# Second pair of layers: eight attention units scored and paired between the value projection's products

## The chip, the cores and the metric

The kernel runs on one core of a Trainium2 chip. The metric is the device time of one execution in microseconds (us); of several runs the median is taken. TensorE (PE) multiplies, VectorE (DVE) and ScalarE (ACT) read its sums from PSUM, GpSimd (POOL) works from SBUF alone, SyncE (SP) starts most transfers.

## The reference, cut to what matters

The program runs two blocks of two layers each. The change touches only the second block, `hybrid_layer`, on 512 positions of 1024 features. Its attention has three kinds of heads: six of kind a (three dilated windows with a bias), four of kind b (the difference of two softmaxes, with a bias), six of kind c (latent queries and keys, with rope).

```
def probs(q, k):                     # kind b
    s = jnp.einsum('bqhd,bkhd->bhqk', sl(q), k) * scale + bias
    return jax.nn.softmax(jnp.where(causal, s, -jnp.inf), axis=-1)
a = probs(q1, k1) - lam * probs(q2, k2)
lam = exp(sum(lf[0] * lf[1])) - exp(sum(lf[2] * lf[3])) + lam_init
out = jnp.einsum('bhqk,bkhd->bqhd', a, v)
```

After attention come the output projection with a layer norm, and a gated feed-forward with a second one. All is in float32.

## The kernel before

Every weight tile is split into a high part (`w_hi`, by ACT, line 759) and a low part (`w_lo`, by POOL, line 705), and each product of a projection is three matmuls (lines 1255 to 1257). SP loads the raw tiles into three slots; a slot is free once its low part is made. There are two slots for split tiles; `split_next()` in ACT's program splits the next tile of a fixed list.

Each engine runs its own program in order and waits on semaphores. A layer of the second block runs so on PE: the projections c, bq, bk and bv; three tiles of a's queries and keys (`("a", j)`), with the transposes of the latent rows among them; a's value projection `("av", kh)`, two halves of four row blocks with 12 matmuls of 384 columns each; the tile `up` (rope queries, c's keys `kn`, the rotation at line 1792, c's queries `qn`, c's values `vc`); the attention loop; the output projection.

The attention loop has 80 units, listed by `units2()`. A unit is one head and one block of 128 queries against n = 128, 256, 384 or 512 keys. Kind b takes two units each, 16 pairs in all. The order is two pairs, then the other 14 pairs spread among 34 units of kinds c and a, then 14 more of a. Of a unit the engines do, each one step or more behind the last:

- PE scores it into one of three PSUM banks, 0, 4 and 6 (line 1838; one matmul for kind b, two for c and a);
- DVE adds the mask or bias strip, writes the buffer `sc2`, and finds the least value (line 2455);
- ACT takes the exponential and its sum (line 1176);
- for the second unit of a pair, DVE scales it and adds the first to it (lines 2465 to 2467);
- four steps after its score PE transposes it (line 1849), ACT copies that to `pt2` (line 1170), and two ranks later PE multiplies it with the values (line 1823); DVE scales the result into `ao` (line 2438).

Banks for the transposes are 2, 1, 3, 5 and 7 in turn. Four of the five `sc2` buffers lie in the high part of the split slot that tile `up` uses, and the fifth in its low part, so the loop cannot write them before `up`'s products are done. Kind c's scores wait for the rope (`s_roped`, DVE line 2407), for the rope keys copied to all heads (`s_kr_all`, POOL lines 733 and 736) and for ACT's copies of `qn` (line 1157).

ACT, before the loop, copies what PE projects: `va` (line 1145), the rope rows (lines 1146 and 1150), then issues six strip loads from its own queue (line 1120), copies `kn` and `qn` (line 1157) and `vc` (line 1160), and takes the exponential for lambda (line 1162). At loop steps 8 and 10 it splits the two halves of the first tile of the output projection. The bias strips of kind b lie in slots 0 to 3 of `strips`, those of kind a in slots 4 to 8, and one in `strips_g`.

Of the kernel before, what the change touches and what calls it, by code (L numbers as in the profile page):

```python
# [16 lines left out]
ALU = mybir.AluOpType  # L17
# [114 lines left out]
def _program(nc, I, out, seen):  # L132
    ctx = ExitStack()
    with ctx:
# [421 lines left out]
        SLOT_ORDER = (3, 0, 2, 1)  # L556

        def units2():
# [40 lines left out]
        STEPS = len(UNITS) + N_B - 1  # L599
        LAST = len(RANKS) - 1  # L600
# [142 lines left out]
        def _(act):  # L743
# [336 lines left out]
            for l in range(DEPTH):  # L1080
# [53 lines left out]
                for j in range(3):  # L1134
                    if j == 2:
                        for i in range(3):
                            act.wait_ge(s_lat.sem, s_lat.at((y, i)))
                            act.activation(cq_hi[:, i, :] if i < 2 else ckv_hi[:], tmp_c[:, i % 2, :], ACT.Copy).then_inc(s_hi.sem, s_hi.nth((y, "c", i)))
                    a_out(2 * j)
                    a_out(2 * j + 1)  # L1140
                    split_next()
                split_next()
# [8 lines left out]
                for h in range(A_HEADS):  # L1151
                    load_strip(h, s_strips)
# [8 lines left out]
                act.wait_ge(s_lam_sums.sem, s_lam_sums.at(y))  # L1161
                act.activation(lam[:, 2:4], lam[:, 0:2], ACT.Exp).then_inc(s_lam_exp.sem, s_lam_exp.nth(y))
                for step in range(STEPS):
# [7 lines left out]
                    if step < len(UNITS):  # L1171
                        u = UNITS[step]
                        n, p_ = u["n"], sc2[step % N_B]
                        total = small[:, 1, step % 8:step % 8 + 1] if u["second"] else sums[:, u["sum"]:u["sum"] + 1]
                        act.wait_ge(s_scored.sem, s_scored.at((y, step)))
                        act.activation(p_[:, 0:n], p_[:, 0:n], ACT.Exp, bias=small[:, 0, step % 8:step % 8 + 1], scale=-1.0,
                                       accum_out=total).then_inc(s_probs.sem, s_probs.nth((y, step)))
# [53 lines left out]
        def _(pe):  # L1231
# [451 lines left out]
            for l in range(DEPTH):  # L1683
# [49 lines left out]
                for j in range(3):  # L1733
# [5 lines left out]
                    if j == 1:  # L1739
                        for i, b in enumerate((5, 7, 0, 2)):  # L1740
# [9 lines left out]
                            m.then_inc(s_lat_t.sem, s_lat_t.nth((y, i)))  # L1750
                for kh in range(2):
# [74 lines left out]
                pe.wait_ge(s_b_lo.sem, s_b_lo.at((y, "bk", 1)))  # L1826
                for step in range(STEPS):
                    if step < len(UNITS):
                        u, b = UNITS[step], S_BANKS[step % N_S]
                        pe.wait_ge(*emptied[b])  # L1830
                        emptied[b] = s_scored.after((y, step))
                        if u["kind"] == "c":
                            pe.wait_ge(s_roped.sem, s_roped.at((y, 1)))
                            pe.wait_ge(s_kr_all.sem, s_kr_all.at((y, u["head"])))
                            pe.wait_ge(s_proj.sem, s_proj.at((y, "qn", 2, 1)))
                        if u["kind"] == "a":
                            pe.wait_ge(s_padded.sem, s_padded.at(y))
                        pe.matmul(ps[:, b, 0:u["n"]], u["q"], u["k"], start=True, stop=True).then_inc(s_scores.sem, s_scores.nth((y, step)))  # L1838
                    r = turns(step)
                    if r is not None:  # L1840
# [7 lines left out]
                        for j in range(len(UNITS[i]["vs"])):  # L1848
                            m = pe.transpose(ps[:, b, P * j:P * j + P], sc2[i % N_B][:, P * j:P * j + P], ident[:])  # L1849
# [107 lines left out]
        def _(dve):  # L1957
# [404 lines left out]
            for l in range(DEPTH):  # L2362
# [35 lines left out]
                m.then_inc(s_lam_sums.sem, s_lam_sums.nth(y))  # L2398
                R = slice(HD, QC)
# [41 lines left out]
                dve.wait_ge(s_strips_b.sem, s_strips_b.at(y))  # L2441
                for st in range(STEPS):
                    if st < len(UNITS):
                        u = UNITS[st]
                        n = u["n"]
                        if st >= N_B and UNITS[st - N_B]["first"]:
                            dve.wait_ge(s_paired.sem, s_paired.at((y, st - N_B + 1)))
                        elif st >= N_B:
# [3 lines left out]
                        if u["kind"] == "a":  # L2452
                            dve.wait_ge(s_strips.sem, s_strips.at(y))
                        dve.wait_ge(s_scores.sem, s_scores.at((y, st)))
                        V.tensor_tensor_reduce(sc2[st % N_B][:, 0:n], ps[:, S_BANKS[st % N_S], 0:n], u["mask"], 1.0, 3.0e38, ALU.add, ALU.min,  # L2455
                                               small[:, 0, st % 8:st % 8 + 1]).then_inc(s_scored.sem, s_scored.nth((y, st)))
                    i = st - 2
                    if st == 2:
                        dve.wait_ge(s_lam_exp.sem, s_lam_exp.at(y))
                        step(V.scalar_tensor_tensor(lam[:, 4:5], lam[:, 3:4], lam[:, 2:3], lam_c[:, 0:1], ALU.subtract, ALU.add))  # L2460
                    if 0 <= i < len(UNITS) and UNITS[i]["second"]:
                        u = UNITS[i]
                        n, ratio = u["n"], small[:, 2, i % 8:i % 8 + 1]
                        dve.wait_ge(s_probs.sem, s_probs.at((y, i)))
                        step(V.reciprocal(ratio, small[:, 1, i % 8:i % 8 + 1]))
                        step(V.tensor_scalar(ratio, ratio, sums[:, u["sum"]:u["sum"] + 1], lam[:, 4:5], ALU.mult, ALU.mult))
                        V.scalar_tensor_tensor(sc2[i % N_B][:, 0:n], sc2[i % N_B][:, 0:n], ratio, sc2[(i - 1) % N_B][:, 0:n],
                                               ALU.mult, ALU.add).then_inc(s_paired.sem, s_paired.nth((y, i)))
# [82 lines left out]
```

## Time and profile before

| | us |
|---|---|
| median of 3 runs | 2019.71 (2019.66 to 2033.64) |
| the profiled execution | 2029.09 |
| its span | 2027.3 |

The profile covers one execution. Times in it run from the start of the span. A row of busy time names an engine and the share of a stretch; PEclk is the clock granted to PE as a share of 2.4 GHz, so 0.50 is 1.2 GHz. A row of the timeline gives the start, the duration, the engine, the line, what is written and read, and in square brackets how long the engine had been idle before and whose work released it. Matmuls overlap at their ends. The attention of the two layers lies at about 849 to 960 us and 1494 to 1605 us.

### The profile page before, as it was taken

The numbers are of one execution on the slowest core, as the hardware profiler recorded it, in microseconds if no ns is written. First come the engines' busy times: TensorE is split into PE (matmuls) and PEld (weight loads), VectorE is DVE, ScalarE is ACT, GpSimd is POOL, SyncE is SP. The second block draws the span as 40 slices with busy tenths as digits, with TensorE's granted clock in tenths as the row PEclk, the third lists the DMA queues.
The fourth block names the chain that finished last, engine by engine and source line by source line (L and its number), as shares of the span: only waits on it lengthen the run. The fifth ranks groups of instructions, "written<-read, shape, count | busy, mean of one in ns | idle before, by whom it ended". The sixth has DMA issues, their size and how long they took to land.

```text
span 2027.3 us, 26898 instructions
## 1 busy us (share of the span) xinstructions
PE 1957.9 (97%) x10454; PEld 1654.0 (82%) x10454; DVE 794.4 (39%) x1830; ACT 827.2 (41%) x1571; POOL 701.1 (35%) x552
## 2 busy tenths in 40 slices
PE   8999999989999999999999999999998999999997
PEld 4898879878779888777888888888877788888886
DVE  3656546452637344367511111027247551111004
ACT  3221268364248456567233222125467523232211
POOL 1523330125450244300544444444420135444441
PEclk9999989999999999999999999999979999999999
DMA  9554320112340024200333333323320133333321
GB/s 275 174 163 149 117 84 2 32 42 83 104 151 33 18 83 126 99 22 16 90 95 92 104 95 114 104 76 104 105 99 1 43 84 104 90 97 104 120 88 42
DMA packets 198117, 183.72 MB, mean 91 GB/s; under 512 B 31686, under 2 KB 166204, under 8 KB 197992
## 3 DMA queue, kind: packets, MB, share of 16 engines
q1 hardware_dynamic: 191960, 170.67, 27.6%
q10 hardware_dynamic: 6032, 11.33, 1.7%
q8 instruction: 85, 1.39, 0.3%
q14 instruction: 40, 0.33, 0.1%
HBM read 179.86 MB, written 5.40 MB: 91 GB/s over the span
## 4 chain that ended last, share of the span: by engine, by line
PE 85%; DVE 6%; ACT 4%; POOL 2%; issue 2%; DMA 1%; ACTq 0%; SPq 0%; DVEq 0%
PE ps L1255 22%; PE ps L1257 22%; PE ps L1256 22%; PE ps L1341 3%; PE ps L1823 3%; PE ps L1838 3%; POOL w_lo L705 2%; PE ps L1849 2%; PE ps L1327 2%; PE ps L1315 2%; PE ps L1372 1%; PE ps L1289 1%; DVE sc L2455 1%; ACT w_hi L759 1%; PE ps L1276 1%
## 5 line engine op out<-in xcount | busy, mean ns | idle before, releaser
L705 POOL TENSOR_TENSOR w_lo<-raw,w_hi 128x512 fp32r<-128x512 f32 (+1 forms) x518 | 679.3, 1343 | 1222.1 <-ACT w_hi L759 1222.0
L759 ACT ACTIVATE w_hi<-raw 128x1024 fp32r<-128x1024 f32 (+2 forms) x261 | 258.2, 1037 | 279.2 <-PE ps L1257 212.7
L1255 PE MATMUL ps<-g_hi,w_lo 128*128 128x512 f32 (+1 forms) x928 | 348.6, 376 | 1.5 <-POOL w_lo L705 1.5
L1256 PE MATMUL ps<-g_lo,w_hi 128*128 128x512 f32 (+1 forms) x928 | 347.7, 375 | 0.0
L1257 PE MATMUL ps<-g_hi,w_hi 128*128 128x512 f32 (+1 forms) x928 | 347.7, 375 | 0.0
L1255 PEld LDWEIGHTS ps<-g_hi,w_lo 128*128 128x128 f32 x928 | 174.7, 188 | 33.7 <-issue 1.7
L1257 PEld LDWEIGHTS ps<-g_hi,w_hi 128*128 128x128 f32 x928 | 174.7, 188 | 31.1
L1256 PEld LDWEIGHTS ps<-g_lo,w_hi 128*128 128x128 f32 x928 | 174.8, 188 | 31.1
L1255 PE MATMUL ps<-h_hi,w_lo 128*128 128x512 f32 (+1 forms) x496 | 180.3, 363 | 4.0 <-DVE h_lo L1972 2.3
L2516 DVE TENSOR_TENSOR tmp_f<-ps,tmp_f 128x512 f32<-128x512 f32 x44 | 30.4, 691 | 370.8 <-PE ps L1257 370.8
L1256 PE MATMUL ps<-h_lo,w_hi 128*128 128x512 f32 (+1 forms) x496 | 174.8, 352 | 0.0
L1257 PE MATMUL ps<-h_hi,w_hi 128*128 128x512 f32 (+1 forms) x496 | 174.7, 352 | 0.0
L1255 PE MATMUL ps<-w_hi,hid_lo 128*128 128x512 f32 x352 | 137.2, 390 | 0.0
L1256 PE MATMUL ps<-w_lo,hid_hi 128*128 128x512 f32 x352 | 137.0, 389 | 0.0
L1257 PE MATMUL ps<-w_hi,hid_hi 128*128 128x512 f32 x352 | 137.0, 389 | 0.0
L1212 ACT ACTIVATE hid_hi<-tmp_f 128x512 fp32r<-128x512 f32 x44 | 27.8, 632 | 237.1 <-DVE tmp_f L2516 237.1
L1255 PE MATMUL ps<-w_hi,g_lo 128*128 128x512 f32 (+3 forms) x320 | 114.3, 357 | 5.3 <-POOL w_lo L705 4.1
L2486 DVE SCALAR_TENSOR_TENSOR res<-res,ps 128x512 f32<-128x512 f32 x32 | 21.9, 684 | 244.9 <-PE ps L1257 244.7
L1257 PE MATMUL ps<-w_hi,g_hi 128*128 128x512 f32 (+3 forms) x320 | 112.9, 353 | 0.0
L1256 PE MATMUL ps<-w_lo,g_hi 128*128 128x512 f32 (+3 forms) x320 | 112.5, 352 | 0.0
L1255 PEld LDWEIGHTS ps<-h_hi,w_lo 128*128 128x128 f32 x496 | 93.9, 189 | 20.8 <-issue 7.3
L1256 PEld LDWEIGHTS ps<-h_lo,w_hi 128*128 128x128 f32 x496 | 94.0, 189 | 14.1 <-issue 2.2
(277 smaller groups left out, 3494.9 us busy)
## 6 DMA issues: line engine op xcount, KB each, us to landing
raw<-in_w_in SPq DMA_DIRECT2D x30, 1024.0 KB, 5.4
raw<-in_w_mod SPq DMA_DIRECT2D x24, 1024.0 KB, 6.4
raw<-in_w_gate SPq DMA_DIRECT2D x44, 512.0 KB, 4.0
raw<-in_w_up SPq DMA_DIRECT2D x44, 512.0 KB, 5.2
raw<-in_w_down SPq DMA_DIRECT2D x22, 1024.0 KB, 4.8
raw<-in_w_out SPq DMA_DIRECT2D x8, 1024.0 KB, 5.0
strips<-bias_rows ACTq DMA_DIRECT2D x18, 256.0 KB, 3.9
raw<-in_w_in SPq DMA_DIRECT2D x16, 256.0 KB, 4.5
```

The costliest lines, as they stand in the source:

```text
L705: pool.tensor_tensor(w_lo[:, i % SPLIT, a:e], raw_of(what)[:, a:e], w_hi[:, i % SPLIT, a:e].bitcast(F32), ALU.subtract).then_inc(s_tile_lo ...
L759: act.activation(w_hi[:, i % SPLIT, a:b], raw_of(what)[:, a:b], ACT.Copy).then_inc(s_tile_hi.sem, s_tile_hi.nth((what, n)))
L1255: pe.matmul(o, lhs[1], rhs[0], start=first, stop=False)
L1256: pe.matmul(o, lhs[0], rhs[1], start=False, stop=False)
L1257: return pe.matmul(o, lhs[0], rhs[0], start=False, stop=last)
L1315: m = pe.matmul(ps_flat[:, o0 + CTX + col:o0 + CTX + col + k.shape[1]], q, k, start=j == 0, stop=j == len(products) - 1)
L1327: m = pe.transpose(ps_flat[:, o0 + P * j:o0 + P * j + P], s_[:, i % n_b, P * j:P * j + P], ident[:])
L1341: m = pe.matmul(ps_flat[:, o0:o0 + HD], turned, v, start=j == 0, stop=j == n - 1)
L1823: m = pe.matmul(ps[:, b, 0:HD], pt2[r % N_P][:, P * j:P * j + P], v, start=j == 0, stop=j == len(u["vs"]) - 1)
L1838: pe.matmul(ps[:, b, 0:u["n"]], u["q"], u["k"], start=True, stop=True).then_inc(s_scores.sem, s_scores.nth((y, step)))
L1849: m = pe.transpose(ps[:, b, P * j:P * j + P], sc2[i % N_B][:, P * j:P * j + P], ident[:])
L2516: V.tensor_tensor(tmp_f[:, 2 + j % 2, :], ps[:, 2 * ((j + 2) % 4) + 1, :], tmp_f[:, j % 2, :], ALU.mult).then_inc(s_glu.sem, s_glu.nth((y, ...
```

## The change

The first four pairs (units 0 to 7, head 0 of kind b) leave the loop. PE scores them behind the row blocks of the value projection, DVE and ACT make and pair their probabilities meanwhile, and these lie in the five strip slots of kind a instead of `sc2`. The exponential for lambda moves ahead of them. The loads of a's strips move from ahead of ACT's `kn` copies into loop steps 14 to 19, one a step, and the split of the output projection's first tile from steps 8 and 10 to 24 and 26. The loop starts at step 5, with units 8, 9 and 10 scored ahead of it; the remaining 12 pairs are spread over the same 34 other units.

```diff
         SLOT_ORDER = (3, 0, 2, 1)
+        EARLY = 8
+        EARLY_AT = (0, 1, 2, 3, 4, 0, 2, 4)
+        EARLY_AMONG = ((0, 1), (2,), (3,), (4,), (5,), (6,), (7,), ())
...
-            u = pairs[0] + pairs[1]
+            u = [x for two in pairs[:EARLY // 2] for x in two]
...
-            for n, two in enumerate(pairs[2:]):
-                upto = (n + 1) * 34 // len(pairs[2:])
+            for n, two in enumerate(pairs[EARLY // 2:]):
+                upto = (n + 1) * 34 // len(pairs[EARLY // 2:])
...
+        FROM = N_B
+        LOADS_FROM = EARLY + N_B + 1
+        def probs_of(i):
+            return strips[:, B_HEADS + EARLY_AT[i], :] if i < EARLY else sc2[i % N_B]
```

ACT (`exp2` is the body of the old loop's exponential, over `probs_of`):

```diff
+                act.wait_ge(s_lam_sums.sem, s_lam_sums.at(y))
+                act.activation(lam[:, 2:4], lam[:, 0:2], ACT.Exp).then_inc(s_lam_exp.sem, s_lam_exp.nth(y))
+                for i in range(EARLY - 4):
+                    exp2(i)
                 split_next()
                 for t in range(XT):
+                    exp2(EARLY - 4 + t)
                     act.wait_ge(s_mm.sem, s_mm.at((y, "av", 1, t)))
...
-                for h in range(A_HEADS):
-                    load_strip(h, s_strips)
...
-                act.wait_ge(s_lam_sums.sem, s_lam_sums.at(y))
-                act.activation(lam[:, 2:4], lam[:, 0:2], ACT.Exp).then_inc(s_lam_exp.sem, s_lam_exp.nth(y))
-                for step in range(STEPS):
+                for step in range(FROM, STEPS):
...
+                    if EARLY <= step < len(UNITS):
+                        exp2(step)
+                    if LOADS_FROM <= step < LOADS_FROM + A_HEADS:
+                        load_strip(step - LOADS_FROM, s_strips)
-                    if step == 8:
+                    if step == 24:
                         split_next((0,))
-                    if step == 10:
+                    if step == 26:
                         split_next((1,))
```

PE (`score(i)` is the body of the old loop's score, with its waits):

```diff
+                pe.wait_ge(s_b_lo.sem, s_b_lo.at((y, "bk", 1)))
                 for kh in range(2):
...
                         m.then_inc(s_mm.sem, s_mm.nth((y, "av", kh, t)))
+                        for i in EARLY_AMONG[XT * kh + t]:
+                            score(i)
...
-                for step in range(STEPS):
-                    if step < len(UNITS):
...
+                for i in range(EARLY, EARLY + N_S):
+                    score(i)
+                for step in range(FROM, STEPS):
+                    if EARLY + N_S <= step < len(UNITS):
+                        score(step)
...
-                            m = pe.transpose(ps[:, b, P * j:P * j + P], sc2[i % N_B][:, P * j:P * j + P], ident[:])
+                            m = pe.transpose(ps[:, b, P * j:P * j + P], probs_of(i)[:, P * j:P * j + P], ident[:])
```

DVE (`scored(i)` and `pair(i)` are the bodies of lines 2455 and 2465 to 2467; this stands ahead of the rope):

```diff
+                dve.wait_ge(s_strips_b.sem, s_strips_b.at(y))
+                for i in range(4):
+                    scored(i)
+                dve.wait_ge(s_lam_exp.sem, s_lam_exp.at(y))
+                step(V.scalar_tensor_tensor(lam[:, 4:5], lam[:, 3:4], lam[:, 2:3], lam_c[:, 0:1], ALU.subtract, ALU.add))
+                for i in range(4, EARLY):
+                    if i > 4:
+                        dve.wait_ge(s_paired.sem, s_paired.at((y, (1, 3, 5)[i - 5])))
+                    scored(i)
+                    pair(2 * (i - 4) + 1)
                 R = slice(HD, QC)
...
-                for st in range(STEPS):
+                for st in range(EARLY, STEPS):
```

## Rows read from the trace of the kernel before

**Rows 1.** The page: span, busy shares, granted clock in 40 slices.

```profile
span 2027.3 us, 26898 instructions
PE 1957.9 (97%) x10454; PEld 1654.0 (82%) x10454; DVE 794.4 (39%) x1830; ACT 827.2 (41%) x1571; POOL 701.1 (35%) x552
PEclk9999989999999999999999999999979999999999
```

**Rows 2.** Busy by stretch: length, PE, PEld, DVE, ACT, POOL; PEclk, DMA, GB/s.

```profile
848.75:854.56 5.81, 2.42 (x8) 1.05 (x7) 4.17 (x13) 5.72 (x15) 3.92 (x6) 1.00 0.00 0
854.56:871.64 17.08, 16.54 (x62) 13.81 (x63) 10.09 (x41) 10.52 (x30) 5.00 (x4) 0.50 0.18 62
871.64:960.35 88.71, 80.50 (x570) 66.67 (x570) 64.44 (x262) 64.17 (x197) 0.00 (x0) 1.00 0.01 1
1493.56:1496.24 2.68, 1.13 (x6) 0.57 (x5) 2.65 (x6) 2.64 (x6) 2.62 (x4) 1.00 0.01 3
1496.24:1516.70 20.46, 19.17 (x66) 14.88 (x67) 11.84 (x50) 13.85 (x40) 6.28 (x7) 0.50 0.14 52
```

**Rows 3.** Timeline of PE where the first attention starts.

```profile
848.75 0.80 PE L1838 MATMUL ps<-bk,bq 128*128 128x512 f32 x3
850.83 0.33 PE L1838 MATMUL ps<-bk,bq 128*128 128x128 f32 x1 [1.28 <-DVE small L2455]
...
855.10 1.12 PE L1849 MATMUL ps<-ident,sc 128*128 128x128 f32 x4 [2.37 <-DVE sc L2467]
```

**Rows 4.** Timeline of DVE: the rope and the first pair.

```profile
841.90 0.69 DVE L2402 TENSOR_TENSOR tmp_c<-ps,sin 128x512 f32<-128x512 f32 x1 [25.98 <-PE ps L1792]
...
847.66 2.38 DVE L2407 TENSOR_TENSOR qc<-qr,tmp_c 32x512 f32<-32x512 f32 x2
...
854.30 0.75 DVE L2467 SCALAR_TENSOR_TENSOR sc<-sc,small,sc 128x512 f32<-128x512 f32 x1
```

**Rows 5.** Timeline of ACT from the last split ahead of the loop.

```profile
827.90 1.90 ACT L759 ACTIVATE w_hi<-raw 128x1024 fp32r<-128x1024 f32 x2 [6.28 <-PE ps L1257]
...
839.00 2.26 ACTq L1120 DMA_DIRECT2D strips<-bias_rows  x5
...
841.78 3.68 ACT L1157 ACTIVATE kc<-ps 64x512 f32<-64x512 f32 x6 [2.20 <-PE ps L1257]
...
849.19 1.64 ACT L1160 ACTIVATE vc<-ps 128x384 f32<-128x384 f32 x4
850.85 1.28 ACT L1162 ACT_TABLE_LOAD   x1
```

**Rows 6.** Busy by stretch, as rows 2: the value projection.

```profile
820.00:836.00 16.00, 16.00 (x94) 16.00 (x93) 0.00 (x0) 5.00 (x8) 8.54 (x7) 1.00 0.25 78
```

**Rows 7.** Lines of DVE: count, ns least/median/most, first and last start, forms.

```profile
L2455 DVE CUSTOM_DVE_ANT_0 sc<-ps,strips x104: 280/486/692, 850.1 to 1593.4; 128x512 f32<-128x512 f32 x26, 128x128 f32<-128x128 f32 x26, 128x384 f32<-128x384 f32 x26, 128x256 f32<-128x256 f32 x26
L2467 DVE SCALAR_TENSOR_TENSOR sc<-sc,small,sc x32: 351/552/752, 854.3 to 1579.5; 128x512 f32<-128x512 f32 x8, 128x128 f32<-128x128 f32 x8, 128x384 f32<-128x384 f32 x8, 128x256 f32<-128x256 f32 x8
```

**Rows 8.** Transfers of b's strips, issued from 787.7: KB each, median us to landing.

```profile
strips<-bias_rows ACTq DMA_DIRECT2D x4, 256.0 KB, 5.3
```

**Rows 9.** Timeline of POOL: low parts of `up`, rope keys.

```profile
829.04 4.75 POOL L705 TENSOR_TENSOR w_lo<-raw,w_hi 128x512 fp32r<-128x512 f32 x4 [4.06 <-ACT w_hi L759]
...
847.71 1.79 POOL L733 TENSOR_TENSOR kc<-qr,tmp_c 32x512 f32<-32x512 f32 x1 [13.92 <-DVE qr L2403]
```

**Rows 10.** Chain that ended last: a c score at full clock.

```profile
877.20 0.91 PE ps L1838 x2
```

**Rows 11.** Busy by stretch, as rows 2, where PE paused elsewhere.

```profile
278.00:282.00 4.00, 0.74 (x5) 0.46 (x4) 4.00 (x11) 3.44 (x8) 1.82 (x1) 0.89 0.37 111
438.00:440.00 2.00, 0.03 (x1) 0.04 (x1) 1.07 (x3) 1.78 (x5) 0.05 (x1) 1.00 0.00 0
610.00:614.00 4.00, 1.79 (x14) 1.38 (x13) 4.00 (x13) 3.64 (x10) 1.55 (x1) 1.00 0.31 66
```

**Rows 12.** Timeline of PE behind the pause at 437 us.

```profile
439.97 1.64 PE L1391 MATMUL ps<-ident,xn 128*128 128x128 f32 x13 [2.84 <-DVE xn L2070]
```

More of the change, by code:

```diff
@@ L1141, in _, with exp2 @@
                     split_next()
+                def exp2(i):
+                    u = UNITS[i]
+                    p_ = probs_of(i)[:, 0:u["n"]]
+                    total = small[:, 1, i % 8:i % 8 + 1] if u["second"] else sums[:, u["sum"]:u["sum"] + 1]
+                    act.wait_ge(s_scored.sem, s_scored.at((y, i)))
+                    act.activation(p_, p_, ACT.Exp, bias=small[:, 0, i % 8:i % 8 + 1], scale=-1.0,
+                                   accum_out=total).then_inc(s_probs.sem, s_probs.nth((y, i)))
+                act.wait_ge(s_lam_sums.sem, s_lam_sums.at(y))
+                act.activation(lam[:, 2:4], lam[:, 0:2], ACT.Exp).then_inc(s_lam_exp.sem, s_lam_exp.nth(y))
+                for i in range(EARLY - 4):
+                    exp2(i)
                 split_next()
                 for t in range(XT):
+                    exp2(EARLY - 4 + t)
                     act.wait_ge(s_mm.sem, s_mm.at((y, "av", 1, t)))
@@ L1750, in _, with score @@
                             m.then_inc(s_lat_t.sem, s_lat_t.nth((y, i)))
+                def score(i):
+                    u, b = UNITS[i], S_BANKS[i % N_S]
+                    pe.wait_ge(*emptied[b])
+                    emptied[b] = s_scored.after((y, i))
+                    if u["kind"] == "c":
+                        pe.wait_ge(s_roped.sem, s_roped.at((y, 1)))
+                        pe.wait_ge(s_kr_all.sem, s_kr_all.at((y, u["head"])))
+                        pe.wait_ge(s_proj.sem, s_proj.at((y, "qn", 2, 1)))
+                    if u["kind"] == "a":
+                        pe.wait_ge(s_padded.sem, s_padded.at(y))
+                    pe.matmul(ps[:, b, 0:u["n"]], u["q"], u["k"], start=True, stop=True).then_inc(s_scores.sem, s_scores.nth((y, i)))
+                pe.wait_ge(s_b_lo.sem, s_b_lo.at((y, "bk", 1)))
                 for kh in range(2):
@@ L2398, in _, with scored, pair @@
                 m.then_inc(s_lam_sums.sem, s_lam_sums.nth(y))
+                def scored(i):
+                    u = UNITS[i]
+                    n = u["n"]
+                    dve.wait_ge(s_scores.sem, s_scores.at((y, i)))
+                    V.tensor_tensor_reduce(probs_of(i)[:, 0:n], ps[:, S_BANKS[i % N_S], 0:n], u["mask"], 1.0, 3.0e38, ALU.add, ALU.min,
+                                           small[:, 0, i % 8:i % 8 + 1]).then_inc(s_scored.sem, s_scored.nth((y, i)))
+                def pair(i):
+                    u = UNITS[i]
+                    n, ratio = u["n"], small[:, 2, i % 8:i % 8 + 1]
+                    dve.wait_ge(s_probs.sem, s_probs.at((y, i)))
+                    step(V.reciprocal(ratio, small[:, 1, i % 8:i % 8 + 1]))
+                    step(V.tensor_scalar(ratio, ratio, sums[:, u["sum"]:u["sum"] + 1], lam[:, 4:5], ALU.mult, ALU.mult))
+                    V.scalar_tensor_tensor(probs_of(i)[:, 0:n], probs_of(i)[:, 0:n], ratio, probs_of(i - 1)[:, 0:n],
+                                           ALU.mult, ALU.add).then_inc(s_paired.sem, s_paired.nth((y, i)))
+                dve.wait_ge(s_strips_b.sem, s_strips_b.at(y))
[8 more added lines that the diff above has]
+                    pair(2 * (i - 4) + 1)
                 R = slice(HD, QC)
@@ L2439, in rows_out2 @@
                                     ALU.mult).then_inc(s_o_out.sem, s_o_out.nth((y, r)))
-                dve.wait_ge(s_strips_b.sem, s_strips_b.at(y))
-                for st in range(STEPS):
+                for st in range(EARLY, STEPS):
                     if st < len(UNITS):
                         u = UNITS[st]
-                        n = u["n"]
-                        if st >= N_B and UNITS[st - N_B]["first"]:
+                        if st >= EARLY + N_B and UNITS[st - N_B]["first"]:
                             dve.wait_ge(s_paired.sem, s_paired.at((y, st - N_B + 1)))
-                        elif st >= N_B:
+                        elif st >= EARLY + N_B:
                             dve.wait_ge(s_turned.sem, s_turned.at((y, UNITS[st - N_B]["rank"])))
@@ L2453, in _ @@
                             dve.wait_ge(s_strips.sem, s_strips.at(y))
[L2454 to L2468, printed above, removed]
+                        scored(st)
+                    if EARLY <= st - 2 < len(UNITS) and UNITS[st - 2]["second"]:
+                        pair(st - 2)
                     if turns(st) is not None and turns(st) >= 3:
```

19 lines of the change are left out of this document (1 added, 18 removed).

## The prediction

> **What bounds the kernel now.** I read the page first: PE is busy for 97% of the span, and its clock is granted in full but for a few slices [rows 1]. So a gain must take idle time or half-clock time from PE, or PE's work itself. The change removes no product, so only the first two are open. The lowest slice, a 7, is the thirtieth (1470 to 1520 us). The busy times by stretch show that it holds the head of layer two's attention, and that layer one's head, which a slice at 9 hides, is the same [rows 2]. Layer one: from 848.75 us PE is busy for 2.42 of 5.81 us; at 854.56 the clock falls to half and stays there for 17.08 us, while PE is busy for 16.54 of them; from 871.64 to 960.35 it is at full clock and busy for 80.50 of 88.71. Layer two has the same order, with 20.46 us at half clock.
>
> The timelines say why. PE ends the last `vc` product and issues three scores; then it idles 1.28 us for the first bank and 2.37 us for the first paired probabilities [rows 3]. DVE cannot take the first score sooner, since it is in the rope until 850.04 (847.66 + 2.38) [rows 4]. ACT is late as well: its `vc` copies end at 850.83, and 1.28 us of table load come before the first exponential [rows 5]. Meanwhile DVE had been idle for 25.98 us before the rope [rows 4]: that is the place into which the change moves work.
>
> **What the head costs in layer one.** From 848.75 to 871.64 are 22.89 us. PE's work in them, in time at full clock, is 2.42 + 16.54/2 = 10.69. Half clock costs 8.27, idle time 3.39 + 0.54 = 3.93. Layer two: 2.68 + 20.46 = 23.14 us, with 1.13 + 19.17/2 = 10.72 of work [rows 2].
>
> **The eight early scores.** They have 2 × (512 + 128 + 384 + 256) = 2560 columns, one matmul each. 94 products of 384 columns fill 16.00 us, 0.17 each [rows 6]; at 320 columns a score that gives 8 × 0.17 × 320/384 = 1.13. Three of them (512, 512, 128) took 0.80 [rows 3], and the other five, none above 384 columns, at most 0.17 each, so no more than 1.65. I take 1.2. They leave the head and lengthen the value projection by the same, so everything behind it starts 1.2 later.
>
> **What hides their other parts.** DVE needs 8 × 0.49 + 4 × 0.55 = 6.1 us by the medians [rows 7], with the small steps behind each some 9 by my estimate, inside its 25.98 idle ones. If that cover were gone, it would delay the rope, and with it c's first score. The b strips were issued at 787.7 and land within some 5.3 us of their issue [rows 8], far ahead of about 822. On ACT the table load and exponentials 0 to 3 stand ahead of the split of `up`. That split started at 827.90 after 6.28 idle us [rows 5]; exponentials 0 and 1 end near 825 and number 3, whose score comes behind the third row block, near 827.5. The split moves only with the products, by about 0.7. Queued behind it are POOL's four low parts, which end at 833.79 [rows 9]; PE reads the first ones at about 836 + 1.2. That leaves more than 3 us. Exponentials 4 to 7 take 0.5 to 0.9 each between `va` copies 2.1 us apart. No PSUM bank is late: bank 0 comes back to PE after three row blocks. I cost all this at nothing.
>
> **The new head.** The `vc` products end at about 849.95 (848.75 + 1.2). PE's next instruction is the score of unit 8, kind c. It needs the rope, at 850.04 + 1.2 = 851.25, and head 0 of the rope keys, at 849.50 + 1.2 = 850.7 [rows 4, 9]; so PE idles 1.3 to 1.4 us. This is the wait that takes the old one's place. Then come that score, 0.91 [rows 10], two short ones, and three transposes of ready probabilities, until 853.5. The first product with the values needs ACT's copy, which can run from 853.1 since the `vc` copies now end near 851.6 (PE ends `vc` at 849.95, ACT copies for 1.64 [rows 5]); this costs 0.1 to 0.3. Idle time in all 1.6. The remaining head work is 10.7 − 1.2 = 9.5 us. Steady state leaves (88.71 − 80.50)/88.71 = 9.3% idle, so 9.5 us of work bring 1.0.
>
> **What moves into the loop.** ACT's queue takes the six strip loads, 2.26/5 = 0.45 each, so 2.7 us; ahead of the loop they held up the `kn` copies until 841.78 [rows 5], and that gap closes, but PE's `qn` and `vc` products and the rope then come last, so it gives nothing. The loads pass nothing on SP's or POOL's queues. They land within microseconds and are first read some 30 steps later. The split is two ACT instructions, some 2.0 us; before it ran in the half-clock stretch. POOL's four low parts behind it, 5 us, come some 15 us later, and SP's refill of that raw slot waits for them; PE first reads this tile at 960, so 80 us cover it. ACT in the loop is busy for 64.17 of 88.71 us, 72% [rows 2], and copies and exponentials queue behind the 4.7 us. Bounds: 0, if ACT catches up in its idle 28%, to 4.7, if all reaches PE. Since the pipeline holds two ranks and four steps between ACT and PE, I take 1.3.
>
> **The sum.** Layer one: 22.89 − (9.5 + 1.6 + 1.0 + 1.3) − 1.2 = 8.3. Layer two: 8.5. Together 16.8. The profiled execution took 2029.09, so it would take 2012.3. It stands 9.4 above the median; the median of 2019.7 becomes 2002.9, say 2003 (−0.8%). With ACT's work wholly hidden the gain is 19.4, to 2000.3; with idle time half of mine too, 22, to 1997.7.
>
> **Does the clock stay up?** Half of the gain hangs on it. At 1496.24 it fell after PE had worked 1.13 of 2.68 us [rows 2], and it fell in 278 to 282 with 0.74 of 4. It stayed up in 610 to 614 with 1.79 of 4, and through an idle time of 2.84 us ahead of 439.97, behind which came only transposes [rows 11, 12]. The new head works some 2.2 of the 3.8 us from 849.95, with one pause of 1.4; that is busier than each of these, so I say it stays up. The Trainium skill, page "TensorE: Matmul & The Clock Gate", section "A second HAM failure mode: psum-queue depth-cycling", speaks against the change: it tells of a kernel whose PE pauses only briefly, but often, between groups of matmuls, and whose clock goes up and down for it. By that the shorter waits of the new head would not be enough. The steady loop, 9.3% idle at a clock of 1.00 over 88.71 us, speaks against that here; no row of before shows the new head itself.
>
> **The rivals.**
> - *The clock falls in both heads after all*, near 853.5, with the same idle times. Of the 9.5 us of work 7.5 then take 15: a head of 2.0 + 15 + 1.6 = 18.6, gain 22.89 − 18.6 − 1.2 = 3.1 and 3.3. Time 2013.3. That is the outcome by the page's rule. In one layer only: 8.4 + 3.2 = 11.6, 2008.1.
> - *The median run of before has no such stretch in one layer*. The runs lie 14 us apart (2019.66 to 2033.64), and the profiled one is 9.4 above the median, which is near the 8.3 to 9.6 that half clock costs in one head. Then the after time is that of the profile, 2012.3.
> - *ACT becomes the bound of the loop head*: 4.7 instead of 1.3 per layer, 6.8 less gain: 2009.7.
> - *The other side: ACT's lateness stops PE, and the clock falls at steps 14 to 26.* The place is the loads and halves of the split. Price: the gain of 8.4, less 3.4 for ACT, less 17 to 20 us at half clock, 8.5 to 10: −3.5 to −5 per layer, some 2028. It decides once PE stands as long as at 278 to 282. Against it: ACT idles 28% there, and PE's longest steady waits are short beside those.
>
> **How the numbers follow.** Forecast (2003, own range 1998 to 2006) 0.42; clock falls in one layer 0.15, in both 0.10; no such stretch in the median run 0.14; ACT the bound 0.09; slower 0.04; better than forecast, because the rarer pairs also leave fewer waits in the loop, 0.06. The range 1997 to 2014 reaches from the better case to the clock falling in both heads; outside are the slower case and half of the better one, and I leave another tenth to the spread of the runs. One per cent is 20.2 us, about what a measurement of this kernel can tell from no change; faster than 1999.5 takes the better case and a third of the forecast's: 0.20. Slower than 2039.9 is reached by no mechanism I can price; I leave 0.03. Within: 0.77.
>
> **What would show it.** In the changed profile: eight b scores at 821 to 836 with no PE idle time around them; DVE busy for some 9 us there; the table load near 822; from 850 one PE wait of 1.3 to 1.4 us released by the rope at line 2407, and none near 2.4 for line 2467; granted clock 1.00 from 850 to 872; the attention ending near 952 instead of 960. A clock of 0.50 after 853 makes the first rival right; PE waits for `pt` or for exponentials near steps 14 to 26 (about 865 to 885) the third.

## The result and the profile after

| | before | after |
|---|---|---|
| median, us | 2025.83 (7 runs, 2017.84 to 2033.94) | 2005.70 (7 runs, 2003.78 to 2009.08) |
| profiled execution, us | 2029.09 | 2004.89 |
| its span, us | 2027.3 | 2003.1 |

The ratio is 0.9903, with a 95% interval of 0.9875 to 0.9932: 1.0% faster. The predicted 2003.0 lies 2.7 below the measured median and the range holds it. By the medians the gain is 20.1 us. The median of before had been 2019.71 over three runs and came to 2025.83 over seven; more on that below.

The page of after, span, shares of PE and granted clock, against [rows 1]:

```profile
span 2003.1 us, 26890 instructions
PE 1940.4 (97%) x10454; PEld 1640.1 (82%) x10454; DVE 797.4 (40%) x1830; ACT 827.4 (41%) x1571; POOL 701.9 (35%) x552
PEclk9999989999999999999999999999999999999999
```

The 7 in slice 30 is gone. Busy time by stretch in after, columns as in [rows 2]: the head's first 3.89 us of layer one, the rest of its attention, the whole, and the stretch from the value projection to the end of `vc`:

```profile
849.99:853.88 3.89, 2.44 (x12) 1.62 (x12) 2.54 (x6) 2.29 (x6) 3.74 (x6) 1.00 0.00 0
853.88:948.37 94.49, 87.40 (x617) 72.46 (x618) 68.47 (x280) 71.52 (x217) 5.16 (x4) 1.00 0.10 29
849.99:948.37 98.38, 89.84 (x629) 74.08 (x630) 71.02 (x285) 73.81 (x222) 8.89 (x10) 1.00 0.10 28
819.15:849.99 30.84, 30.84 (x160) 27.51 (x158) 16.11 (x39) 21.11 (x42) 10.37 (x8) 1.00 0.23 77
```

The clock is 1.00 throughout, where [rows 2] has 17.08 us at 0.50. The loop takes 98.38 us instead of 111.60, and PE's idle time in it is 98.38 − 89.84 = 8.54 instead of some 12.1. PE has no idle time at all in the stretch into which the scores went.

Timeline of PE in after, the first and last early scores and the head, against [rows 3]:

```profile
821.23 0.63 PE L1781 MATMUL ps<-bk,bq 128*128 128x512 f32 x2
...
834.89 0.28 PE L1781 MATMUL ps<-bk,bq 128*128 128x256 f32 x1
...
851.20 1.10 PE L1781 MATMUL ps<-kc,qc 96*128 96x512 f32 x2 [1.21 <-DVE qc L2463]
851.73 1.03 PE L1781 MATMUL ps<-bk,bq 128*128 128x512 f32 x2
852.60 1.04 PE L1876 MATMUL ps<-ident,strips 128*128 128x128 f32 x8
853.88 1.10 PE L1858 MATMUL ps<-vb,pt 128*128 128x64 f32 x8 [0.25 <-ACT pt L1192]
...
858.29 0.66 PE L1876 MATMUL ps<-ident,sc 128*128 128x128 f32 x4 [0.66 <-DVE sc L2442]
```

Timeline of ACT in after, against [rows 5]: the table load lies at 821.40, under the value projection, and the split of `up` starts half a microsecond later than before.

```profile
821.40 1.28 ACT L1164 ACT_TABLE_LOAD   x1
...
828.39 1.90 ACT L770 ACTIVATE w_hi<-raw 128x1024 fp32r<-128x1024 f32 x2 [1.31 <-PE ps L1276]
...
850.02 1.64 ACT L1184 ACTIVATE vc<-ps 128x384 f32<-128x384 f32 x4 [0.90 <-PE ps L1276]
```

**A measure for the experiments.** The whole time of an execution varies by what the clock does, also in the first block, which no kernel here changes. So each layer is also measured by itself, along the chain of work that ended last in the profiled execution: from the first transpose of the latent rows, ahead of the value projection, to the last transpose ahead of the output projection. In the chain of before and in that of after, for layer one:

```profile
806.88 1.31 PE ps L1747 x12
...
959.47 0.88 PE ps L1813 x8
```

```profile
806.64 1.31 PE ps L1766 x12
...
947.49 0.88 PE ps L1848 x8
```

Before: 959.47 + 0.88 − 806.88 = 153.47. After: 948.37 − 806.64 = 141.73. Layer two: 153.63 and 142.12. These 11.74 and 11.51 are 23.3 of the 24.2 us between the profiled executions. In two executions more of the changed kernel the measure was 141.75 and 142.08, 141.71 and 142.11, so it repeats to 0.1 as long as the clock does not fall in it.

Where the clock falls, one profile does not tell what the next execution does. Take the pause of [rows 12] in the first block: in all fourteen profiles behind this text PE waits there for 2.84 to 2.86 us. The clock stays up behind it in four of them (before, after, b_moved, a_bfirst_r) and falls for 3.4 us in the other ten. Timeline of PE and busy time in a_again:

```profile
438.92 2.18 PE L1410 MATMUL ps<-ident,xn 128*128 128x128 f32 x13 [2.86 <-DVE xn L2097]
```

```profile
436.00:446.00 10.00, 7.14 (x32) 6.11 (x32) 5.42 (x9) 8.32 (x15) 5.46 (x4) 0.83 0.07 9
```

Of before there is one profile, of an execution with a mean granted clock of 0.984 and 37.6 us of half clock in the two heads. The executions of before with 0.991 have some 36 us of half clock in all (my estimate, 0.009 × 2 × 2016), and the fourteen profiles have 17 to 33 outside the heads. So such an execution had at most some 20 us in its heads. Each layer time with a fall in it, that of before too, is one draw.

| kernel | median us | ratio to before (95%) | layer one, two, us | half clock in the two heads, us |
|---|---|---|---|---|
| before | 2025.8 | | 153.47, 153.63 | 17.1, 20.5 |
| changed | 2005.7 | 0.9903 (0.9875 to 0.9932) | 141.73, 142.12 | 0, 0 |
| b_fill | 2016.8 | 0.9964 (0.9941 to 0.9987) | 147.82, 147.82 | 0, 0 |
| b_moved | 2021.4 | 0.9982 (0.9958 to 1.0006) | 153.94, 153.89 | 17.1, 17.1 |
| b_order | 2016.8 | 0.9955 (0.9934 to 0.9975) | 149.47, 149.47 | 13.6, 10.2 |
| b_lam | 2017.1 | 0.9956 (0.9931 to 0.9981) | 149.05, 149.00 | 10.2, 6.8 |
| a_split8 | 2002.8 | 0.9882 (0.9849 to 0.9914) | 141.66, 142.03 | 0, 0 |
| a_rope3 | 2011.5 | 0.9928 (0.9899 to 0.9958) | 146.13, 145.09 | 6.8, 3.4 |
| a_again | 2003.3 | 0.9890 (0.9863 to 0.9917) | 141.75, 142.08 | 0, 0 |
| a_bfirst8 | 2022.8 | 0.9980 (0.9959 to 1.0001) | 155.12, 149.44 | 30.7, 17.0 |
| a_bfirst | 1999.7 | 0.9875 (0.9835 to 0.9915) | 140.13, 140.48 | 0, 0 |
| a_turn | 2003.5 | 0.9894 (0.9849 to 0.9939) | 140.79, 141.13 | 0, 0 |
| a_bfirst_r | 2002.8 | 0.9894 (0.9860 to 0.9928) | 140.14, 140.51 | 0, 0 |
| a_again_r | 2003.5 | 0.9896 (0.9862 to 0.9930) | 141.71, 142.11 | 0, 0 |

The last two columns are those of the profiled execution; the half-clock times are summed from the granted clock in stretches of 2 us. Each ratio goes by runs of before taken beside that kernel. Their median was 2023.6 beside b_fill, b_moved, a_split8 and a_rope3, 2028.9 beside b_order, b_lam, a_again and a_bfirst8, 2029.4 beside a_bfirst and a_turn, and 2027.6 beside the last two. Each of b_fill, b_order, b_lam and a_rope3 is faster than before clear of noise, and b_moved and a_bfirst8 cannot be told from it.

### The profile page after: what moved, and what is told of

Read it like the earlier page. It is cut to its first block, busy times and chain, and to the rows that moved or that the text cites. A ratio compares the mean times of both kernels' runs of the same rounds, so it can differ in the third digit from the quotient of the medians.

```text
span 2003.1 us, 26890 instructions
## 1 busy us (share of the span) xinstructions
PE 1940.4 (97%) x10454; PEld 1640.1 (82%) x10454; DVE 797.4 (40%) x1830; ACT 827.4 (41%) x1571; POOL 701.9 (35%) x552
## 4 chain that ended last, share of the span: by engine, by line
PE 85%; DVE 7%; ACT 3%; POOL 2%; issue 2%; DMA 0%; SPq 0%; ACTq 0%; DVEq 0%
PE ps L1274 23%; PE ps L1276 23%; PE ps L1275 23%; PE ps L1360 3%; PE ps L1781 2%; PE ps L1858 2%; POOL w_lo L716 2%; PE ps L1346 2%; PE ps L1334 2%; PE ps L1876 1%; PE ps L1391 1%; DVE sc L2432 1%; PE ps L1308 1%; ACT w_hi L770 1%; PE ps L1295 1%
```

## The experiments

**Theory**: more than half of the gain is the clock, which fell because TensorE paused in the head; the rest is waits. **Rivals**: the gain is the waits alone; it is the strip loads moved away from in front of `kn`; it is the new order of the units.

### The clock alone: b_fill

The kernel before, with matmuls that nobody reads in the two pauses.

```diff
+                def fill(n):
+                    pe.wait_ge(*emptied[7])
+                    for _ in range(n):
+                        pe.matmul(ps[:, 7, :], bq[:, 0, 0:P], bk[:, 0, :], start=True, stop=True)
                 for step in range(STEPS):
+                    if step == 3:
+                        fill(4)
+                    if step == N_B:
+                        fill(9)
```

> The kernel before, with 4 and 9 matmuls of 512 columns into a free bank put into TensorE's two waits at the head of each attention; nothing reads them. Theory (most of the gain is the clock): TensorE has no long pause, the granted clock stays at 1.00 through both heads, and of the 8.3 and 9.6 us that half clock costs there some 1 each comes back as waits on DVE and ACT; 14 to 16 us faster than before, while DVE's and ACT's late start stays. Rival (the gain is the waits taken away, the clock follows other work): within 2 us of before, or slower by the matmuls. Clock 1.00 but under 8 us faster: half clock hid waits that come back.

Timeline of PE in b_fill, and its attention of layer one by stretch:

```profile
849.13 1.19 PE L1832 MATMUL ps<-bk,bq 128*128 128x512 f32 x4 [0.52 <-DVE qc L2418]
...
851.04 2.61 PE L1832 MATMUL ps<-bk,bq 128*128 128x512 f32 x9
...
854.17 0.66 PE L1860 MATMUL ps<-ident,sc 128*128 128x128 f32 x4 [0.35 <-DVE sc L2478]
854.58 0.42 PE L1849 MATMUL ps<-bk,bq 128*128 128x384 f32 x1
854.84 0.43 PE L1849 MATMUL ps<-kc,qc 96*128 96x128 f32 x2
856.03 0.33 PE L1860 MATMUL ps<-ident,sc 128*128 128x128 f32 x1 [0.76 <-DVE sc L2478]
```

```profile
847.80:953.74 105.94, 95.17 (x651) 77.50 (x651) 78.58 (x314) 80.03 (x241) 9.07 (x10) 1.00 0.03 11
```

The clock stays up, and the layers gain 5.65 and 5.81 us, 11.5 in all against this one profile of before: half of the change's 23.3. I had expected 14 to 16. Half clock hid more waits than the 1 us a layer that I allowed: it cost 8.3 and 9.6 us of PE's time, and 2.6 and 3.8 of that came back as idle time, as in the last rows above, where PE at full clock catches up with DVE's pairing again at once. By the ratio the gain is 0.36%; the single runs of this kernel, too, lie between 2014.8 at a mean granted clock of 0.995 and 2025.1 at 0.988. The rival by which only waits count is out, but so is my split: the clock alone, taken first, is half, not more. The share depends on what is taken first, since a pause that is gone leaves less half clock and half clock leaves shorter pauses. In all, PE's attention of layer one is 13.2 us shorter in after than in before, 9.6 of them busy time (99.46 to 89.84) and 3.6 idle time (12.14 to 8.54).

### The loads and the split alone: b_moved

```diff
-                for h in range(A_HEADS):
-                    load_strip(h, s_strips)
...
+                    if 14 <= step < 14 + A_HEADS:
+                        load_strip(step - 14, s_strips)
-                    if step == 8:
+                    if step == 24:
                         split_next((0,))
-                    if step == 10:
+                    if step == 26:
                         split_next((1,))
```

> The kernel before, with one part of the change alone: the six strip loads at loop steps 14 to 19 and the two halves of the split at steps 24 and 26. Theory: ACT starts the kn copies 1 us sooner, but TensorE's head waits for the rope and for the table load; within 2 us of before, clock falls as before. Rival (the loads in front of kn were the point): 3 us or more faster. Rival (ACT becomes the bound in the loop): 3 us or more slower.

The layers are 0.47 and 0.26 us longer, the interval of the ratio holds 1, and the clock falls as before. Both rivals are out. ACT's earlier `kn` copies bring nothing, because its `qn` and `vc` copies then wait for PE's products: the `vc` copies start 42.07 us behind the first transpose of the latent rows, against 42.31 in before. The moved work costs at most half a microsecond a layer.

### ACT's work back at the head: a_split8

```diff
-                    if step == 24:
+                    if step == 8:
                         split_next((0,))
-                    if step == 26:
+                    if step == 10:
                         split_next((1,))
```

> The changed kernel with the two halves of the split back at steps 8 and 10, where ACT has the queue of the head before it. If ACT's 2.0 us reach TensorE there: 2 to 4 us slower than the changed kernel. If ACT catches up: within 1 us of it. Clock stays 1.00 in both.

The layers take 141.66 and 142.03, against 141.75 and 142.08 in a_again: ACT catches up. PE waits 1.26 us for its first pairing instead of 0.66, and the loop takes that back later.

### The order alone: b_order

Four pairs lead the loop of before; nothing is scored early. ACT waits for the rope and the rope keys at step 5, since its copies now come sooner and lie where the rope's rows were.

```diff
-            u = pairs[0] + pairs[1]
+            u = [x for two in pairs[:4] for x in two]
...
-            for n, two in enumerate(pairs[2:]):
-                upto = (n + 1) * 34 // len(pairs[2:])
+            for n, two in enumerate(pairs[4:]):
+                upto = (n + 1) * 34 // len(pairs[4:])
```

> The kernel before with the new order of units alone: four pairs at the front of the loop instead of two, the other 12 spread over the same 34. Nothing is scored early. Rival (the fewer waits for pairs in the loop, 4.5 to 2.9 us a layer, come from the order): 2 to 4 us faster than before. Theory (the early scores and their cover are the gain): within 3 us of before or slower, since DVE meets four pairs in a row behind the rope; the clock falls as before.

The layers are 4.0 and 4.2 us shorter, more than either side said, and the kernel is faster than before clear of noise. The clock still falls, but for 23.8 us in both heads instead of 37.6. In layer one PE's busy time in the attention goes from 99.46 to 96.67 us, which is less half clock, and its idle time from 12.14 to 10.92. So the order itself takes 1.2 us of waits from layer one; whether it or the execution makes the half clock shorter is not shown. The last pause was no shorter: this timeline of PE in b_order has 3.03 us where [rows 3] has 2.37.

```profile
848.16 0.33 PE L1841 MATMUL ps<-bk,bq 128*128 128x128 f32 x1 [1.26 <-DVE small L2458]
848.78 0.65 PE L1841 MATMUL ps<-bk,bq 128*128 128x384 f32 x2 [0.29 <-DVE small L2458]
852.46 1.11 PE L1852 MATMUL ps<-ident,sc 128*128 128x128 f32 x4 [3.03 <-DVE sc L2470]
```

But that pause is not what brought the clock down. The clock was at 1.00 until 849.3 and at 0.50 from then on, as the first scores ended; the pause of 3.03 us lies behind that. Ahead of the fall stand only the waits of 1.26 and 0.29 for the first bank. Busy time in b_order from the first score to the fall, columns as in [rows 2]:

```profile
846.10:849.30 3.20, 1.65 (x7) 0.93 (x6) 2.80 (x7) 3.16 (x6) 3.14 (x5) 1.00 0.00 0
```

### The table load alone: b_lam

The exponential for lambda moves ahead of the split of `up`, as in the change, and nothing else.

```diff
+                act.wait_ge(s_lam_sums.sem, s_lam_sums.at(y))
+                act.activation(lam[:, 2:4], lam[:, 0:2], ACT.Exp).then_inc(s_lam_exp.sem, s_lam_exp.nth(y))
                 split_next()
                 for t in range(XT):
...
-                act.wait_ge(s_lam_sums.sem, s_lam_sums.at(y))
-                act.activation(lam[:, 2:4], lam[:, 0:2], ACT.Exp).then_inc(s_lam_exp.sem, s_lam_exp.nth(y))
```

> The kernel before with lambda's exponential, and so the table load of 1.28 us, moved ahead of the value projection's copies, alone. The first exponential can start at 850.8 instead of 852.2, and the first pair 1.2 us sooner. Theory: 2 to 3 us faster if only the pause shrinks and the clock still falls; 10 us or more if the shorter pause of TensorE keeps the clock up.

```profile
849.55 0.33 PE L1838 MATMUL ps<-bk,bq 128*128 128x128 f32 x1 [1.24 <-DVE small L2455]
850.16 1.13 PE L1838 MATMUL ps<-kc,qc 96*128 96x512 f32 x2 [0.28 <-DVE small L2455]
852.39 1.11 PE L1849 MATMUL ps<-ident,sc 128*128 128x128 f32 x4 [0.85 <-DVE sc L2467]
```

In this timeline of PE in b_lam the 2.37 us of [rows 3] are 0.85. The clock falls all the same, for 10.2 and 6.8 us, and the layers gain 4.42 and 4.63. That is neither of the two amounts expected. In layer one it falls at 851.2, ahead of the 0.85, behind waits of 1.24 and 0.28 alone:

```profile
847.48:851.20 3.72, 2.19 (x8) 1.05 (x7) 3.35 (x11) 3.70 (x10) 3.66 (x6) 1.00 0.00 0
```

The changed kernel has waits of 1.21 and 0.25 in its head, with 2.44 us of work in 3.89, and its clock stayed up in both heads of all three profiles. What separates these two cases is not shown.

Moving this one exponential gains 9.1 of the change's 23.3 us, and b_order's order alone 8.2. If the two added up, they would give 17.2 without any early score. No run has both, so what the early scoring brings by itself is not isolated.

### The wait that is left, made longer: a_rope3

```diff
                     dve.wait_ge(s_rot.sem, s_rot.at((y, g)))
+                    if g == 0:
+                        for _ in range(3):
+                            step(V.tensor_tensor(tmp_c[0:n, g, :], ps[0:n, ROTB[g], :], sin2[0:n, :], ALU.mult))
```

> The changed kernel with three more DVE products (0.7 us each) in front of each rope, so that the one wait left in the head grows from 1.2 to about 3.4 us. Theory (the clock falls when TensorE's pause there is long enough): the clock falls in at least one head, and the kernel is 12 to 24 us slower than the changed one. Rival (only the waits count): 4.4 us slower, 2.2 a layer.

PE's wait becomes 3.07 us, in the head of layer one and in that of layer two:

```profile
851.20 2.05 PE L1781 MATMUL ps<-kc,qc 96*128 96x512 f32 x2 [3.07 <-DVE qc L2466]
```

```profile
1487.03 1.10 PE L1781 MATMUL ps<-kc,qc 96*128 96x512 f32 x2 [3.07 <-DVE qc L2466]
```

The clock falls in both heads, so this wait, made longer, is enough to undo what the change does for the clock. It comes back after 6.8 and 3.4 us, not after 17 to 20. The cost is 4.4 and 3.0 us by layer: 1.86 is the wait, and 3.4 and 1.7 are half of the half-clock time, less 0.9 and 0.6 that PE gains back. I had expected 12 to 24 in all; by the medians it is 8.7 more than a_split8 beside it.

### The wait filled: a_bfirst8, a_bfirst, a_turn

Three kernels put work into the changed kernel's wait of 1.21 us. `turned(step)` is the body of PE's loop from the transposes on; ACT gets the same wait for the rope as in b_order.

```diff
-                u += others[done:done + half] + two + others[done + half:upto]
+                u += two + others[done:upto] if n == 0 else others[done:done + half] + two + others[done + half:upto]
...
-                for i in range(EARLY, EARLY + N_S):
+                for i in range(EARLY, EARLY + 2):
                     score(i)
-                for step in range(FROM, STEPS):
+                for step in (5, 6, 7):
+                    turned(step)
+                for i in range(EARLY + 2, EARLY + N_S):
+                    score(i)
+                for step in range(8, STEPS):
```

That is a_bfirst; a_bfirst8 has the split halves at steps 8 and 10 besides.

> The changed kernel with the wait of 1.2 us in each head filled: units 8 and 9 are a pair of kind b, which does not wait for the rope, and are scored at once; the transposes of units 1 and 3 come before the score of the first c unit; ACT waits for the rope by itself before it overwrites its rows. The split halves are at steps 8 and 10 again. Theory (the rope wait is on the path): 2 to 3 us faster than the changed kernel. Rival (DVE and ACT behind the rope are the path, TensorE only catches up): within 1 us of it.

The layers are 13.4 and 7.3 us longer than the changed kernel's, with more half clock in the heads, 47.7 us, than in any other profile here. Timelines of PE and DVE in a_bfirst8:

```profile
853.72 0.66 PE L1875 MATMUL ps<-ident,sc 128*128 128x128 f32 x4 [2.23 <-DVE sc L2452]
```

```profile
852.10 1.57 DVE L2452 SCALAR_TENSOR_TENSOR sc<-sc,small,sc 128x512 f32<-128x512 f32 x1
```

PE no longer waits for the rope; it comes early to the first pairing instead and waits 2.23 us there. Ahead of that pairing ACT has split a half of the tile, and the pairing itself takes 1.57 us instead of the 0.75 of [rows 4], while POOL makes the low parts. The clock falls at 855.1, behind that wait, for 30.7 us.

> The kernel of the run with the b pair first, but with the split halves left at steps 24 and 26. If ACT's two split halves and POOL's low parts behind them (which made the first pairing of DVE 1.57 us long and let TensorE wait 2.2 us for it) were what brought the clock down: the clock stays at 1.00, and the kernel takes 1 to 3 us less than the changed one, 2000 to 2002. If the order itself leaves DVE and ACT behind: the wait and the low clock remain, over 2010.

With the halves at steps 24 and 26 the pairing takes 0.75 and PE waits 0.52 for it; the clock stays at 1.00:

```profile
853.63 0.66 PE L1875 MATMUL ps<-ident,sc 128*128 128x128 f32 x4 [0.52 <-DVE sc L2452]
```

The layers take 1.6 us less than the changed kernel's, each. So the change's move of the split, worth nothing by itself (a_split8), is what makes this step safe. ACT's half and POOL's low parts were moved together, but the timelines part them. Counted from each kernel's first transpose of the latent rows, the pairing starts 0.9 us later in a_bfirst8 (852.10 − 803.17 against 852.82 − 804.78), since DVE waits 0.80 us for ACT's exponential ahead of it, and it then lasts 0.8 longer. The two make up the 1.7 by which PE waits longer.

a_turn leaves the order of the units and only takes the transposes ahead of the scores.

> The changed kernel with the transposes of units 1 and 3 ahead of the score of unit 8, so that 0.55 us of ready work fill part of the 1.2 us wait for the rope. If TensorE is the path in the head: 1 to 1.6 us faster. If the next pair's probabilities are (DVE line 2442, on which it waits 0.66 us right behind): within 0.5 us, that wait grows to 1.2 or more.

The layers are 0.94 and 0.99 us shorter, so the head is TensorE's path; the wait for the next pairing stays at 0.66.

### The best version beside the changed one: a_again, a_bfirst_r, a_again_r

> The changed kernel once more, on the chip and in the rounds of the three that follow, as what they are compared with. 0.990 of before as measured first; if the part of the clock varies by chip, 0.986 to 0.994.

> The kernel with the b pair first and the split at steps 24 and 26 once more, in the same rounds as the changed kernel. If its one earlier measurement (1999.7, against 2003.3 of the changed kernel on another chip) holds: 2 to 4 us below the changed kernel here, and the same difference between executions with the same granted clock. If that was the chip: within 1 us.

> The changed kernel, to compare the former with: 2002 to 2006 us, granted clock 0.989 to 0.995.

In the same rounds the medians are 2002.83 and 2003.53, a difference of 0.7. The two layers together are 3.2 us shorter, as in the first measurement, but the profiled execution of a_bfirst_r has 10.2 us of half clock at 282 to 294, in the first block, where that of a_again_r has 3.4. So a_bfirst is shorter where it differs; that it is the faster program by more than 1 us is not shown. By executions with the same mean clock it is 0.4 to 2.0 us faster at 0.993 (three against one) and 3.8 at 0.992 (one against one), too few to settle it.

## Why the prediction was right, and what it mis-sized

**The mechanism** was as forecast, step by step: no PE idle time in the value projection; DVE busy for 8.5 us between 821 and 836; the table load near 822 (821.40); one wait of 1.2 us for the rope's line; the clock at 1.00. Only the attention ended still earlier than the 952 that I gave, at 948.

**The sizes**, for layer one, where the sum gave 8.3 and the measure 11.7:

- *Eight early scores*, 1.2: the `vc` products now end 1.3 us later behind the anchor (849.65 − 806.64 against 848.58 − 806.88). Right.
- *The new waits*, 1.6: 1.21 + 0.25 = 1.46. Right.
- *ACT's moved work*, 1.3 taken out of 0 to 4.7: it costs nothing in a_split8, where only the split is moved back, and at most half a microsecond in b_moved. This term failed. I had read the 2.26 us of [rows 5] as time in which ACT does nothing else. In after, issues take 0.33 each and lie under ACT's own work:

```profile
858.87 0.40 ACT L1160 ACTIVATE sc<-sc,small 128x128 f32<-128x128 f32 x1 [0.66 <-DVE small L2432]
859.09 0.33 ACTq L1131 DMA_DIRECT2D strips<-bias_rows  x1
859.18 0.19 ACT L1160 ACTIVATION_READ_ACCUMULATOR sc<-sc,small 128x1 f32 x1
```

- *Steady idle time*, 9.3% or 9.2 us: 8.54 − 1.46 = 7.1 us. This is the larger miss, 2.1 us. I had carried the share of idle time over as it was and added 1.0 for the head's work. But the loop now has 12 pairs instead of 14 among the same other units, and waits for pairings are a large part of it. Waits of PE behind the head, in before, after and b_order (who waited, for whom, us, times, longest):

```profile
PE ps L1849 <- DVE sc L2467: 4.5, 7, 1.0
PE ps L1849 <- DVE ao L2438: 3.4, 7, 0.8
```

```profile
PE ps L1876 <- DVE ao L2494: 4.0, 9, 0.8
PE ps L1876 <- DVE sc L2442: 2.9, 5, 0.9
```

```profile
PE ps L1852 <- DVE ao L2441: 4.0, 9, 0.8
PE ps L1852 <- DVE sc L2470: 2.0, 4, 0.9
```

The waits for pairings fall from 4.5 to 2.9 us and those for `ao` rise by 0.6. b_order has the same with nothing scored early, so this is the order of the units.

With these 1.3 + 2.1 + 0.1 (the new waits were 1.46 instead of 1.6) the 8.3 becomes 11.8, against 11.74.

**Two errors cancelled**, and that the forecast lies within 2.7 us is luck to that extent. The gain in terms of the profiled execution was 24.2, not 16.8; but the median of before, from which I subtracted, was 6 us too low. From the median over seven runs my 16.8 would have given 2009.0, 3.3 above the measured one. Among the runs of before measured beside these kernels, those with a mean granted clock of 0.991 take 2017.4 to 2018.7, those with 0.984 mostly 2028 to 2030, those with 0.980 some 2033. The changed kernel's seven runs lie within 5.3 us, its six of a_again within 7.5. A part of the gain is thus that executions with a low mean clock are gone. Where both kernels have executions with the same mean clock, 0.989 and 0.990, the changed one takes 7 to 15 us less. That range is an estimate of what the gain is without the clock. The rival "the median run has no such stretch in one layer" had this right for single runs of before, not for its median.

**The clock** was given as half of the gain; b_fill says 11.5 of 23.3. But my sum got there by wrong parts: 8.3 to 9.6 us a layer for the clock, less 1.0 of waits that come back, where 2.6 to 3.8 come back; and 2.3 for the waits, where early scores, table load, cover and order together bring 6.1. The rival with the clock falling in both heads was priced at some 5 us a layer for the fall. The runs show no one price: 2.5 and 1.1 in a_rope3 beyond its longer wait, 15.0 and 9.0 in a_bfirst8 against a_bfirst, its longer wait included.

My reason for the clock to stay up does not hold, though it did stay up. I compared the new head, 2.2 us of work in 3.8, with emptier places. In b_lam the clock fell after 2.19 in 3.72. And behind the pause of 2.84 us at 437, where I had seen it stay up, it falls in ten of fourteen profiles. That the clock stays up in the changed head is measured; that I foresaw it is in part luck. The Trainium skill, page "TensorE: Matmul & The Clock Gate", section "A second HAM failure mode: psum-queue depth-cycling", tells of a clock that goes up and down because PE pauses briefly and often. The traces of b_lam and b_order agree, with waits of 1.24 and 0.28 and of 1.26 and 0.29 us ahead of the fall in layer one; the changed kernel, with 1.21 and 0.25, does not show it.

**Open**: what ends a stretch at half clock. It lasted 3.4 to 30.7 us in these heads, 6.8 and 10.2 us in b_lam behind short pauses and 3.4 and 6.8 in a_rope3 at one of 3.07. No run here tells what decides it, or why the same pause brings the clock down in one execution and not in another. So such a stretch could not be priced from the pause ahead of it.

## What to carry to other kernels

Where a loop's first items wait for engines that still finish the stage before it, look for idle time of those engines one stage earlier and for dead buffers to hold the results: here 25.98 idle us of DVE and the strip slots not yet loaded. Count the granted clock at the seam as a cost of its own, but measure it with matmuls that nobody reads in the pauses, since half clock also hides waits that come back. Read the clock from more than one profile, since the same pause can bring it down in one execution and not in the next. Try the cheap parts of a change alone: here the table load moved by itself gave some two fifths of what the layers gained. And before filling a remaining wait, look at what the engine will meet next: the same fill gained 1.6 us a layer or lost 7 to 13, by whether another engine's unrelated work stood in front of the next result.

## What the runs showed of the hardware

DVE's pairing (two operands and the result in SBUF) of 512 columns takes 0.75 us by itself, and 1.71 when POOL makes low parts at the same time, as in these timelines of DVE and POOL in after; reads from PSUM (line 2432) beside it keep their 0.56 for 384 columns.

```profile
828.67 0.56 DVE L2432 CUSTOM_DVE_ANT_0 strips<-ps,strips 128x384 f32<-128x384 f32 x1 [1.99 <-PE ps L1781]
...
829.66 1.71 DVE L2442 SCALAR_TENSOR_TENSOR strips<-strips,small 128x512 f32<-128x512 f32 x1
831.40 0.56 DVE L2432 CUSTOM_DVE_ANT_0 strips<-ps,strips 128x384 f32<-128x384 f32 x1
...
832.39 0.35 DVE L2442 SCALAR_TENSOR_TENSOR strips<-strips,small 128x128 f32<-128x128 f32 x1
...
833.97 1.32 DVE L2442 SCALAR_TENSOR_TENSOR strips<-strips,small 128x384 f32<-128x384 f32 x1
```

```profile
829.52 5.35 POOL L716 TENSOR_TENSOR w_lo<-raw,w_hi 128x512 fp32r<-128x512 f32 x4 [4.78 <-ACT w_hi L770]
```

The Trainium skill, page "GPSIMD Engine Reference", section "1. Specifications", says that GpSimd contends with VectorE instructions that read two inputs from SBUF; the trace agrees for the larger pairings, 1.71 against 0.75 us for 512 columns and 1.32 against 0.62 for 384, and for POOL's four parts, 5.35 against 4.75 [rows 9]. The pairing of 128 columns kept its 0.35 beside POOL. The forecast had cover for it, 5.56 idle us of DVE behind the last early pair.
